# A two-block transformer kernel on one core: new column addresses, one factor turned by transposes, and four mixing pieces at other places

## What is computed

```
def second-block layer(x):                 # cut to what matters here
    p = rmsnorm(x) @ w_in                  # columns of the branches and of three gates
    y0 = rwkv7_branch(p)                   # state recurrence, per head and token:
        # S_t = S_{t-1} (diag(w_t) - kk_t^T (a_t kk_t)) + v_t^T k_t ;  y_t = S_t r_t
        # then a group norm, a bonus term, a gate
    y1 = retention_branch(p); y2 = sgu_branch(p)
    x = x + (sum_b sigmoid(gate_b) * (y_b @ w_branch_b)) @ w_out
    x = x + conv_ffn(rmsnorm(x))           # up, depthwise conv of width 3, silu(gate)*value, down
```

## Time and profile before

| | |
|---|---|
| time, median of 3 | 2283.04 us |
| profiled execution | 2291.36 us, its span 2289.6 us |
| TensorE matmuls busy | 2189.4 us |
| VectorE busy | 1409.1 us |
| ScalarE busy | 1002.0 us |
| mean granted clock of TensorE | 0.98 |

### The profile page before, as it was taken

How to read it: one execution, slowest core, us unless ns; L and a number is a source line. 1 busy time by engine, 2 the same in 40 slices (tenths; PEclk the granted TensorE clock), 3 DMA queues, 4 the chain that set the end, 5 groups by cost and what they waited for, 6 DMA issues and landing times. The chain is left out here.

```text
span 2289.6 us, 39101 instructions
## 1 busy us (share of the span) xinstructions
PE 2189.4 (96%) x16210; PEld 2049.0 (89%) x16210; DVE 1409.1 (62%) x2091; ACT 1002.0 (44%) x1409; POOL 18.8 (1%) x18
## 2 busy tenths in 40 slices
PE   7999999999999999999999899899999989989998
PEld 7999987999999997899889799889988979988997
DVE  6555366655744656755575766576767576657775
ACT  4434266433533445633364333355445433335443
POOL 0000000000000000000000100000000010000000
PEclk9999899999999999999999899999999989999999
DMA  8435332553554522544443223365534322336551
GB/s 306 191 144 192 122 121 93 221 212 148 200 207 169 191 93 84 200 188 164 165 158 111 79 84 103 99 248 196 184 114 164 106 80 87 102 94 247 203 184 47
DMA packets 79579, 349.08 MB, mean 152 GB/s; under 512 B 21200, under 2 KB 30544, under 8 KB 45520
## 3 DMA queue, kind: packets, MB, share of 16 engines
q1 hardware_dynamic: 79440, 347.07, 42.0%
HBM read 345.99 MB, written 1.05 MB: 152 GB/s over the span
## 5 line engine op out<-in xcount | busy, mean ns | idle before, releaser
L89 PE MATMUL bank<-ffn_hT_split,n_split_gate_up 128*128 128x256 f32 x1408 | 392.0, 278 | 2.8 <-DVE ffn_hT_split L192 2.4
L90 PE MATMUL bank<-ffn_hT_split,n_split_gate_up 128*128 128x256 f32 x1408 | 391.9, 278 | 0.0
L91 PE MATMUL bank<-ffn_hT_split,n_split_gate_up 128*128 128x256 f32 x1408 | 391.4, 278 | 0.0
L89 PEld LDWEIGHTS bank<-ffn_hT_split,n_split_gate_up 128*128 128x128 f32 x1408 | 265.6, 189 | 5.3 <-issue 3.6
L90 PEld LDWEIGHTS bank<-ffn_hT_split,n_split_gate_up 128*128 128x128 f32 x1408 | 265.6, 189 | 1.5
L91 PEld LDWEIGHTS bank<-ffn_hT_split,n_split_gate_up 128*128 128x128 f32 x1408 | 265.1, 188 | 0.0
L1787 DVE TENSOR_TENSOR mix_parts<-mix_arrived,mix_parts 128x1024 fp32r<-128x1024 f32 x88 | 107.4, 1224 | 137.5 <-ACT mix_parts L1782 137.2
L356 ACT ACTIVATE work<-bank 128x256 f32<-128x256 f32 x88 | 33.2, 382 | 314.9 <-PE bank L91 314.7
L454 DVE TENSOR_TENSOR work<-bank,work 128x256 f32<-128x256 f32 x88 | 37.2, 423 | 197.0 <-ACT work L356 197.0
L435 DVE TENSOR_TENSOR ffn_split_down<-ffn_arrived_down,ffn_split_down 128x2048 fp32r<-128x2048 f32 x44 | 100.8, 2291 | 85.4 <-ACT ffn_split_down L351 85.4
L417 DVE TENSOR_TENSOR n_split_gate_up<-arrived_gate_up,n_split_gate_up 128x2048 fp32r<-128x2048 f32 x64 | 144.7, 2287 | 12.5 <-ACT n_split_gate_up L341 12.5
(11 more groups left out here) (383 smaller groups left out, 6160.7 us busy)
## 6 DMA issues: line engine op xcount, KB each, us to landing
arrived_gate_up<-in_ffn SPq DMA_DIRECT2D x64, 1024.0 KB, 8.6
ffn_arrived_down<-in_ffn SPq DMA_DIRECT2D x44, 1024.0 KB, 4.9
mix_arrived<-in_mix_w SPq DMA_DIRECT2D x88, 512.0 KB, 3.6
rrived_gate_up<-in_conv_ffn SPq DMA_DIRECT2D x32, 1024.0 KB, 6.9
_arrived_gate_up<-in_ffn SPq DMA_DIRECT2D x24, 1024.0 KB, 6.7
mixer_arrived<-in_w_in SPq DMA_DIRECT2D x22, 1024.0 KB, 6.8
onv_ffn_arrived_down<-in_conv_ffn SPq DMA_DIRECT2D x22, 1024.0 KB, 4.8
irst_project_arrived<-in_w_in SPq DMA_DIRECT2D x17, 1024.0 KB, 4.9
```

What stands on the lines that cost most here:

```text
L89: pe.matmul(out, lhs[0], rhs[0], start=start, stop=False)
L90: pe.matmul(out, lhs[0], rhs[1], start=False, stop=False)
L91: return pe.matmul(out, lhs[1], rhs[0], start=False, stop=stop)
```

## The change

**Addresses.** The transposed activations and their neighbours of the first map move by 32 columns (`hT` 0 to 32) and slot 0's weights with them; slot 1's weights stay. In the second map the weights of projection and mixing move by 56 columns, and the convolution feed-forward's activations from 18576 to 18560 with its weights to 80 and 36560. Sizes and the order of use are the same.

**The transposed inverse.** outer(n) makes one product only. Two steps later `turn_inverse(n)` transposes the new z quad on TensorE (L2810 of the kernel after) and ScalarE's `copy_inverse(n)` writes x. VectorE's second addition is gone. outer(n) waits for the copy of four steps earlier.

**Pieces.** TensorE runs pieces 2 and 3 ahead of score(1, 2) and score(1, 3); their follow-ups stay at steps 0 and 1. Pieces 22 and 23 leave the steps: `TAIL` = 22 takes the place of `FIRST_GATE0` in the code after the recurrence, which now has ten pieces where it had eight. One stands before `turn_y(0)`'s transposes and one behind `turn_y(1)`'s more than before. On VectorE, keep(0, 1) comes before the normalizing, and scale(1) ahead of `turned_low(0)`.

```diff
-    c.ffn = FfnMemory(at, "ffn", dict(hT=0, act=4096, arrived_down=6144, arrived=(blocks(9168, 2), blocks(23152, 2)),
-                                      parts=(blocks(13264, 2, 2), blocks(27248, 2, 2)), down_parts=blocks(35440, 2, 2)))
-    c.hT_parts = at("mixer_T_parts", 0, [P, 2, KT, S], F32R)
+    c.ffn = FfnMemory(at, "ffn", dict(hT=32, act=4128, arrived_down=6176, arrived=(blocks(9200, 2), blocks(23152, 2)),
+                                      parts=(blocks(13296, 2, 2), blocks(27248, 2, 2)), down_parts=blocks(35440, 2, 2)))
+    c.hT_parts = at("mixer_T_parts", 32, [P, 2, KT, S], F32R)
...
     c.units_parts = [[at(f"rw_project_parts{n}_{lo}", col, [P, UNIT], F32R)[:] for lo, col in enumerate(cols)]
-                     for n, cols in enumerate(((24216, 26264), (28312, 34456), (30360, 32408)))]
+                     for n, cols in enumerate(((24272, 26320), (28368, 34512), (30416, 32464)))]
...
-    c.half_parts = [at(f"mix_parts{n}", col, [P, 2, HALF_UNIT], F32R) for n, col in enumerate((30360, 32408, 24216))]
+    c.half_parts = [at(f"mix_parts{n}", col, [P, 2, HALF_UNIT], F32R) for n, col in enumerate((30416, 32464, 24272))]
...
-    c.conv_ffn = FfnMemory(at, "conv_ffn", dict(hT=18576, act=40600, arrived=(blocks(8192, 2), blocks(26264, 2)), arrived_down=12288,
-                                                parts=(blocks(0, 2, 2), ((36504, 38552), (24216, 34456))),
-                                                down_parts=((14480, 16528), (30360, 32408)), taps=22672))
+    c.conv_ffn = FfnMemory(at, "conv_ffn", dict(hT=18560, act=40656, arrived=(blocks(8272, 2), blocks(26320, 2)), arrived_down=12368,
+                                                parts=(blocks(80, 2, 2), ((36560, 38608), (24272, 34512))),
+                                                down_parts=((14464, 16512), (30416, 32464)), taps=22672))
...
-    AT_STEP = {0: 2, 1: 3, **{n: n for n in range(4, TOTAL)}}
+    TAIL = FIRST_GATE0 - 2
+    AT_STEP = {0: 2, 1: 3, **{n: n for n in range(4, TAIL)}}
...
+        def copy_inverse(n):
+            act.wait_ge(s["x_turned"], n + 1)
+            act.activation(quad(x, n % QUADS), bank4(6 + n % 2), ACT.Copy).then_inc(s["x_copied"], 1)
...
             if n + 1 < TOTAL:
                 copy_inner(n + 1)
+            if 2 <= n < BOTH + 2:
+                copy_inverse(n - 2)
...
-            if n < BOTH:
-                dve.tensor_tensor(quad(x, q), quad(x, q), bank4(6 + n % 2), ALU.add).then_inc(s["updated"], 1)
...
+            if n >= QUADS:
+                pe.wait_ge(s["x_copied"], n - QUADS + 1)
             for i in range(4):
                 last = pe.matmul(c.ps[4 + n % 2][:, i * P:(i + 1) * P], x[:, 4 * q + i],
                                  inner[:, n % 2, i * P:(i + 1) * P], start=True, stop=True)
-            if n < BOTH:
-                for i in range(4):
-                    last = pe.matmul(c.ps[6 + n % 2][:, i * P:(i + 1) * P], inner[:, n % 2, i * P:(i + 1) * P],
-                                     x[:, 4 * q + i], start=True, stop=True)
...
+        def turn_inverse(n):
+            pe.wait_ge(s["updated"], n + 1)
+            if n >= 2:
+                pe.wait_ge(s["x_copied"], n - 1)
+            for i in range(4):
+                last = pe.transpose(c.ps[6 + n % 2][:, i * P:(i + 1) * P], z[:, 4 * (n % QUADS) + i], c.ident)
+            last.then_inc(s["x_turned"], 1)
...
-            if n in AT_STEP:
+            if n in AT_STEP and n >= QUADS:
                 piece(AT_STEP[n])
```

More of the change, by code:

```diff
@@ L1739, in second_map @@
     c.rhs0 = at("rw_rhs", LOCAL + 9216, [P, RW_W])
[L1740 to L1744, removed]
-    c.half_parts = [at(f"mix_parts{n}", col, [P, 2, HALF_UNIT], F32R) for n, col in enumerate((30360, 32408, 24216))]
+    c.z = at("inverse", 37584, [P, UNITS, P])[:]
+    c.low = at("level_rows", 39632, [P, 2, 512])
+    c.a_rows = at("a_rows", 34512, [P, UNITS, P])[:]
+    c.y_parts = at("branches_T", 26320, [P, 2, 2, 4, S], F32R)
+    c.half_arrived = [at(f"mix_arrived{n}", col, [P, HALF_UNIT])[:] for n, col in enumerate((40656, 41680, 36560))]
+    c.half_parts = [at(f"mix_parts{n}", col, [P, 2, HALF_UNIT], F32R) for n, col in enumerate((30416, 32464, 24272))]
     c.y_rw_parts = at("rw_T_parts", 7208, [P, 2, 4, S], F32R)
     c.merged_parts = at("merged_parts", LOCAL, [P, 2, KT, S], F32R)
-    c.conv_ffn = FfnMemory(at, "conv_ffn", dict(hT=18576, act=40600, arrived=(blocks(8192, 2), blocks(26264, 2)), arrived_down=12288,
-                                                parts=(blocks(0, 2, 2), ((36504, 38552), (24216, 34456))),
-                                                down_parts=((14480, 16528), (30360, 32408)), taps=22672))
+    c.conv_ffn = FfnMemory(at, "conv_ffn", dict(hT=18560, act=40656, arrived=(blocks(8272, 2), blocks(26320, 2)), arrived_down=12368,
+                                                parts=(blocks(80, 2, 2), ((36560, 38608), (24272, 34512))),
+                                                down_parts=((14464, 16512), (30416, 32464)), taps=22672))
 R_, K_, V_, A_, LW, KK, BH, KH, KR, KR2, E1, E2 = range(12)
@@ L2331, in turned_high @@
             act.activation(c.y_rw_parts[:, 0, :, t * P:(t + 1) * P], bank4(2 + t), ACT.Copy).then_inc(s["rw_high"], 1)
-        after(FIRST_GATE0)
+        after(TAIL)
         copy_w(0)
-        after(FIRST_GATE0 + 1)
-        after(FIRST_GATE0 + 2)
+        after(TAIL + 1)
+        after(TAIL + 2)
         act.wait_ge(s["rhs_ready"], 2)
         act.activation(rhs[1], c.ps[7][:], ACT.Copy).then_inc(s["rhs_copied"], 1)
-        after(FIRST_GATE0 + 3)
+        after(TAIL + 3)
         copy_w(1)
@@ L2342, in scalar @@
         root(0)
-        after(FIRST_GATE0 + 4)
+        after(TAIL + 4)
         square(1)
         root(1)
-        after(FIRST_GATE0 + 5)
+        after(TAIL + 5)
+        after(TAIL + 6)
         turned_high(0)
-        after(FIRST_GATE0 + 6)
-        after(FIRST_GATE0 + 7)
+        after(TAIL + 7)
+        after(TAIL + 8)
         turned_high(1)
+        after(TAIL + 9)
         def merged_high(p):
@@ L2444, in vector @@
         decay(3)
+        keep(0, 1)
         dve.wait_ge(s["sg_rooted"], 1)
@@ L2569, in vector @@
         sum_squares(1)
-        after(FIRST_GATE0 + 5)
+        after(TAIL + 5)
+        scale(1)
+        after(TAIL + 6)
         turned_low(0)
-        scale(1)
-        after(FIRST_GATE0 + 6)
-        after(FIRST_GATE0 + 7)
+        after(TAIL + 7)
+        after(TAIL + 8)
         turned_low(1)
+        after(TAIL + 9)
         for p in range(KT // 2):
@@ L2754, in tensor @@
         score(1, 1)
+        piece(2)
         score(1, 2)
+        piece(3)
         score(1, 3)
@@ L2817, in w_product @@
             last.then_inc(s["w_ready"], 1)
-        piece(FIRST_GATE0)
+        piece(TAIL)
         pe.wait_ge(s["inner_copied"], TOTAL)
         w_product(0)
-        piece(FIRST_GATE0 + 1)
+        piece(TAIL + 1)
         pe.wait_ge(s["w_copied"], 1)
@@ L2840, in tensor @@
                       start=(u == NH), stop=False, skip_group_check=True)
-        piece(FIRST_GATE0 + 2)
+        piece(TAIL + 2)
         pe.wait_ge(s["state_copied"], 1)
@@ L2849, in tensor @@
                       start=False, stop=False, skip_group_check=True)
-        piece(FIRST_GATE0 + 3)
+        piece(TAIL + 3)
         w_product(1)
-        piece(FIRST_GATE0 + 4)
+        piece(TAIL + 4)
         pe.wait_ge(s["w_copied"], 2)
@@ L2857, in tensor @@
         last.then_inc(s["y_ready"], 1)
-        piece(FIRST_GATE0 + 5)
+        piece(TAIL + 5)
+        piece(TAIL + 6)
         def turn_y(t):
@@ L2866, in tensor @@
         turn_y(0)
-        piece(FIRST_GATE0 + 6)
-        piece(FIRST_GATE0 + 7)
+        piece(TAIL + 7)
+        piece(TAIL + 8)
         turn_y(1)
+        piece(TAIL + 9)
         for m in range(FIRST_BR0, N_HALF_UNITS - RING):
```

29 lines of the change are left out of this document (14 added, 15 removed).

## The result

The changed kernel takes 2229.82 us (median of 4, 2227.59 to 2231.51) against 2283.07 for the one before: ratio 0.9764, 95% interval 0.9738 to 0.9791, or 53 us less. 2210 was forecast, a gain of 73.

The account below looks back on a forecast made before the run. TensorE, busy 96% of the span, was taken as the bound. Per layer 11.0 + 6.2 + 6.8 = 24, two layers 48, addresses 25, together 73, from the median 2283.04 to 2210 us; range 2190 to 2243.

Parts of the forecast that it names:

- The new addresses: Hidden chunks, mixer, projection and gates: all at distance 16 modulo 64, so 113.3 ns a matmul; 25 us.
- Convolution feed-forward: Its hidden chunks: 2 x 10 chunks x 0.46 us faster at distance 16; 9.2 us.
- Plain feed-forwards: Slot 1's slow hidden chunks become fast: 4 phases x 4 chunks x 0.42 us; 6.7 us.
- Mixer, projection and gates: Their matmuls reach 113.3 ns at distance 16: 3 us for the mixer, 2 projection, 4.5 gates.
- rivals 1: Whole kernel: addresses have no effect, the schedule works as worked out; 2235 us, chance 0.17.
- Rival 2: Head and tail: gaps only move and the clock falls as before; 14 a layer, with addresses 2230 us, chance 0.15.
- The turned inverse: Recurrence steps from piece 4 on: transposes replace a matmul group, steps 5.07 us from 5.52; net 6.2 us a layer.
- The head: Up to piece 4: earlier keep, pieces 2 and 3 in gaps, no half clock, steps 0 to 3 lighter; 11.0 us a layer.
- The tail: After the last state product: pieces 22 and 23 cover waits, 4.5 us, clock stays up, 2.3; 6.8 us a layer.
- The schedule as a whole: Scan-and-mix phases: head, transposed inverse and tail together 24 us a layer, 48 in two layers.
- Rival 3: Feed-forward chunks: addresses spoil the fast slot, +12 us with nothing gained; 2247 us, chance 0.07.
- Rival 4: Recurrence: the clock falls inside the steps, +162 us; 2372 us, slower than before, chance 0.03.

Follow-up runs that it names:

- hidden48: Changed kernel with all hidden chunks and all down-projections of the feed-forwards at column distance 48 modulo 64; 2238.12 us, 0.9805 of the kernel before.
- conv_down0: Changed kernel with both halves of the convolution feed-forward's down-projection at column distance 0 modulo 64, from 16 and 0; 2226.39 us, 0.9738 of the kernel before.
- down0_48: Changed kernel with the down-projection at column distance 0 modulo 64 in the four plain feed-forwards, 48 in the convolution one; 2233.53 us, 0.9775 of the kernel before.
- down48_tail: Changed kernel with the convolution's down-projection at distance 48 in both halves and ScalarE's high part for piece TAIL+8 made earlier; 2215.90 us, 0.9702 of the kernel before.
- down16: Changed kernel with the down-projection at column distance 16 modulo 64 in all feed-forwards; 2233.43 us, 0.9780 of the kernel before.
- sched_only: Kernel before with the new order of work and transposed inverse, but the old addresses; 2243.18 us, 0.9822 of the kernel before.
- addr_only: Kernel before with only the two memory-map functions of the changed kernel; 2272.50 us, 0.9933 of the kernel before.

## Why the prediction was right in kind and 20 us too far

**The new addresses: the step that failed.** "After the change all of these have 16 [...] So I expect 113.3 ns in all" gave 25 us; the addresses alone measured 15 (10 to 20).
- Convolution feed-forward, 9.2 forecast: 0.4 and 0.5 between the traces. Nearly the whole miss of this part. I had read that its slot 0 is slow at 48 and fast elsewhere at 16, and named the distance as the cause. The row for it was misread: 1529.71:1541.05 is chunk 1, so slot 1, whose distance was 8 (36504 - 18576). Slot 0 was slow too, at 117.8 ns, but only behind the first down-projection; its chunk 0, at the same 48, ran at 114.2. The distance does count (hidden48), but behind each chunk runs a down-projection with its own, and with a half or all of its weights at 0 the next chunk was slow at each own distance seen (16 in conv_down0, 48 and 8 in before). With 48 there it is fast (down0_48, down48_tail).
- Plain feed-forwards, 6.7 forecast: a phase that runs fast takes 192.3 where it took 194.5, 2.2 less; a slow one 0.8 to 2.4 more. With one slow phase in four, as seven of the nine traces with (16, 48) there have it, an execution gets about 5. Part of it is the downs, 5.52 us in this kernel; they had no term.
- The alternation of the earlier trace rows was the right thing to ask about, but I gave it to the slots' distances alone. A down at 16 makes chunks of equal distance alternate too (down16). In before and sched_only it was slot 1, the one at 48, that was slow in all eight phases, so the slot's distance may have had its share; no run parts the two. The clue stood in the earlier trace rows: chunk 1 was fast until the first down-projection. I wrote that 48 "can be fast but does not stay so", and didn't ask what had run in between.
- Mixer, projection and gates, 9.5 forecast. Projections 2.4 and 1.0 less, steps 0.95 less a layer in addr_only; the mixer's weight-standing stretch 17.06 in one layer and 16.43 in the other. About 6 in these traces. The mixer's stretch has two paces as well: of its 24 instances in the twelve traces with the new addresses 17 are fast and 7 slow, of the four with the old ones all are slow.

The two paces of one shape at one clock, 10.88 and 11.31 us for 96, moved by the columns of the buffers alone (conv_down0 and down0_48 differ in where the feed-forwards' middle activations stand, and the buffer behind them in the plain ones, and in no instruction), are shown. Why the columns matter is not: no run looks into how the operands are read. The Trainium skill (TensorE: Matmul & The Clock Gate, Step-by-step: what each phase is for) says that a weight load doesn't take read bandwidth from the running matmul; by that this part would have given 0 where it gave 15.

That rivals 1 (addresses inert, 2235) and 2 (gaps only move, 2230) came closer than the forecast is chance. Rival 2 has the measured time to the microsecond, but takes the addresses at 25 and the head and tail at 8 a layer, where the addresses gave 15, and TensorE's waits shrank from 7.1 to 0.9 us in the head and from 6.6 to 2.8 in the tail.

**The turned inverse: right.** 5.07 us a step forecast, 5.05 measured; no wait for a copied inverse. Undoing it cost 16 us, 8 a layer, against 6.2 and the 1.8 of the head's four groups.

**The head: right by the traces.** 11.0 a layer forecast, 10.8 and 11.4 found. Recurrence start 4.8 us sooner (4.7 forecast), one wait for keep of 0.9 (1.5), waits of inner(3) and inner(4) 0.6 and 0.9 (0.9 and 1.4). By medians undoing it costs 15, not 18: how far the clock falls in the head without the change varies (62.26, 57.81), and one trace had it fall with the change.

**The tail: mechanism right, size too large.** The wait of 2 us for the ring was there (2.1), the branch pieces ran at full clock. But I had taken the clock to stay up because the two long waits were gone; behind the 2.1 us wait that is left it fell for 3.4 us, which cost 1.7. 6.8 a layer forecast; 4.0 by undoing it in the trace, 7 by medians, whose interval is 5 us to each side for both layers.

**The schedule as a whole:** 48 forecast, 41 (35 to 46) measured; head, turned inverse and tail undone one at a time cost 15 + 16 + 14 = 45. The 7 us missing here and the 10 of the addresses are most of the 20. Rival 2 (gaps only move, 14 a layer) is refuted by the waits. Rival 3 (the fast slot is spoiled) came in small: in the one slow phase of four the chunks of slot 0, fast before, are slow too, some 5 x 0.42 = 2 us. Rival 4 didn't happen: steps ran at 1.00 with 0.44 us of transposes in each 5.05. By the Trainium skill (TensorE: Matmul & The Clock Gate, Part 4: PE-mode transpose) the full clock doesn't engage for transposes, which don't count as busy the way matmuls do; no run here shows whether that is so, only that this share of them did no harm among matmuls.

## What to carry to other kernels

When equal matmuls run at two paces by turns, don't ask only which operand differs; ask what ran between the two, and undo each of the two alone before giving the change a price. A wait of 2 us on TensorE cost nearly twice its length here (3.7 us), since the clock fell behind it: look for the in-order instruction that stands needlessly ahead of what TensorE waits for (here a table load ahead of a copy). Take an edit's size from more than one trace of a kernel, since a single one was 4 to 9 us longer in one stage than any of the other thirteen.

## What the runs showed of the hardware that I had not expected

- A run of equal 256-column matmuls has two paces, 113.6 and 117.8 ns a matmul, at the same granted clock of 1.00. Which one it gets depends on the operands' column distances (16 or 48, modulo 64), on those of the matmuls before it (0, 16 or 48), and for chunks at 16 with downs at 16 or 48 on the execution.
- With chunks at 16 and downs at 48, six of the eleven phases that began at 118.2 ns were fast behind their first down-projection and five stayed slow.
- 512-column matmuls: 226.7 ns at distance 0, some 229 at 48, 233 at 16, about 235 with 16 and 0 mixed.
- A wait of TensorE of 2.1 us was followed by 3.4 us at half clock, and with the wait taken away the clock stayed at 1.00.
